# Expert rounds in narrow-wide pairs, with two small reorderings, in a one-core two-block transformer kernel

## The reference

```python
# first block, layer 0: hyena on 512 channels, order 2, by FFT-like convolutions
y_hy = hyena_mixer(z[..., :3 * C_HYENA], *hy)
# first block, layer 1: top 2 of 8 experts for each token
x = x + gt2 * moe_swiglu(modulate(rmsnorm(x, g_ffn), sh2, sc2), w_router[j], b_router[j],
                         moe_w1[j], moe_w3[j], moe_w2[j])
# second block, layer 0: retention, 4 heads of 512 values, normalised head by head
mu = jnp.mean(o, axis=-1, keepdims=True)
oc = o - mu
o = oc * lax.rsqrt(jnp.mean(oc * oc, axis=-1, keepdims=True) + EPS)
return (jax.nn.silu(g) * o) @ w_out
```

## Time and profile before

| | us |
|---|---|
| three runs | 2678.87, 2681.10, 2684.21 (median 2681.10) |
| the profiled execution's own time | 2679.57 |
| its span in the profile | 2677.8 |
| PE busy / DVE / ACT / POOL | 2458.1 / 1268.9 / 848.3 / 217.6 |
| transfers of expert weights | 340 of 1024 KB |

### The profile page before, as it was taken

The page is one execution under the profiler, slowest core; times in us unless marked ns, Lnnn a source line. Parts: engine busy times, 40 slices in busy tenths (PEclk is TensorE's granted clock), DMA queues, the critical chain, the costliest instruction groups (busy, mean ns, idle before and its releaser), DMA issues.

```text
span 2677.8 us, 39073 instructions
## 1 busy us (share of the span) xinstructions
PE 2458.1 (92%) x15909; PEld 1664.4 (62%) x15909; DVE 1268.9 (47%) x1936; ACT 848.3 (32%) x1213; POOL 217.6 (8%) x247
## 2 busy tenths in 40 slices
PE   7998999999887887889998998998989998899998
PEld 2864769954332322325776776777857996654996
DVE  3306645523310101005665755757455767895664
ACT  2101544421000000003554554554423544101553
POOL 0401200001000000000000000000000007362000
PEclk9998999999999999999998998999999999999999
DMA  8727275567999999998765765766556655534452
GB/s 297 172 79 266 26 260 176 187 265 281 382 411 412 410 414 409 411 414 302 260 229 188 255 220 191 265 207 219 190 218 209 218 187 179 199 126 134 158 184 84
DMA packets 248153, 648.75 MB, mean 242 GB/s; under 512 B 12623, under 2 KB 102896, under 8 KB 225656
## 3 DMA queue, kind: packets, MB, share of 16 engines
q10 hardware_dynamic: 111760, 358.68, 35.7%
q1 hardware_dynamic: 130648, 275.51, 29.7%
q0 software_dynamic: 5584, 12.28, 2.4%
HBM read 645.38 MB, written 1.05 MB: 241 GB/s over the span
## 4 chain that ended last, share of the span: by engine, by line
PE 75%; DMA 15%; DVE 6%; issue 2%; ACT 1%; POOL 1%; ACTq 1%; SPq 0%; POOLq 0%; DVEq 0%
DMA ring<-in_moe_w 13%; PE bank L1535 6%; PE bank L700 5%; PE bank L1553 5%; PE bank L1554 5%; PE bank L1552 5%; PE bank L702 4%; PE bank L701 4%; PE bank L1562 4%; PE bank L1563 4%; PE bank L1564 4%; PE bank L715 3%; PE bank L633 2%; PE bank L1596 2%; PE bank L667 2%; PE bank L1984 2%
## 5 line engine op out<-in xcount | busy, mean ns | idle before, releaser
L1074 DVE TENSOR_TENSOR w_low<-ring,w_high 128x1024 fp32r<-128x1024 f32 x252 | 305.5, 1224 | 129.0 <-ACT w_high L868 126.8
L633 PE MATMUL bank<-ring,arena 128*64 128x512 f32 (+1 forms) x1280 | 267.3, 548 | 71.1 <-DMA ring<-in_moe_w 71.1
L868 ACT ACTIVATE w_high<-ring 128x1024 fp32r<-128x1024 f32 x252 | 265.3, 1058 | 197.0 <-PE bank L702 195.4
L2459 DVE TENSOR_TENSOR ring_low<-ring,up_high 128x1024 fp32r<-128x1024 f32 x186 | 227.0, 1278 | 113.3 <-ACT up_high L2101 112.9
L1552 PE MATMUL bank<-ht_low,up_high 128*128 128x256 f32 x960 | 272.9, 284 | 0.0
L633 PEld LDWEIGHTS bank<-ring,arena 128*64 128x64 f32 x1280 | 81.9, 136 | 252.4 <-DMA ring<-in_moe_w 151.0
L2101 ACT ACTIVATE up_high<-ring 128x1024 fp32r<-128x1024 f32 x186 | 182.5, 1046 | 84.3 <-PE bank L1564 73.0
L1058 DVE TENSOR_TENSOR HT<-HT,bank 128x512 f32<-128x512 f32 (+1 forms) x20 | 12.4, 622 | 374.6 <-PE bank L633 374.6
L1553 PE MATMUL bank<-ht_high_cf_up,up_high 128*128 128x256 f32 x640 | 183.0, 286 | 0.0
L1552 PEld LDWEIGHTS bank<-ht_low,up_high 128*128 128x128 f32 x960 | 180.3, 188 | 1.6 <-DVE arena L2335 0.8
L1554 PE MATMUL bank<-ht_high_cf_up,ring_low 128*128 128x256 f32 x640 | 181.1, 283 | 0.0
(11 more groups left out here) (424 smaller groups left out, 4218.9 us busy)
## 6 DMA issues: line engine op xcount, KB each, us to landing
ring<-in_moe_w ACTq DMA_DIRECT2D x340, 1024.0 KB, 14.3
ring<-in_w_ada SPq DMA_DIRECT2D x48, 1024.0 KB, 7.7
ring<-in_ada_w SPq DMA_DIRECT2D x48, 1024.0 KB, 5.0
ring<-in_ffn_w_up SPq DMA_DIRECT2D x44, 1024.0 KB, 5.1
ring<-in_ffn_w SPq DMA_DIRECT2D x33, 1024.0 KB, 5.4
ring<-in_ret_w_in SPq DMA_DIRECT2D x24, 1024.0 KB, 5.2
ring<-in_ffn_w_down SPq DMA_DIRECT2D x22, 1024.0 KB, 4.9
ring<-in_w_in SPq DMA_DIRECT2D x12, 1024.0 KB, 11.2
```

The source lines that it names most:

```text
L633: mm = pe.matmul(PS[b][64 * n:64 * n + 64, 0:cols], XGF[:, ks * h + k, :], w[:, k, cols * n:cols * n + cols], start=h + k == 0, stop=ks * ...
L868: act.activation(WH[half % SPLIT][:, :], slot(moe_first + i)[:, HALF * (half % 2):HALF * (half % 2) + HALF], ACT.Copy)\
L1074: dve.tensor_tensor(out=WL[half % SPLIT][:, :], in0=slot(i)[:, HALF * (half % 2):HALF * (half % 2) + HALF], in1=WH[half % SPLIT][:, :], op ...
L2459: dve.tensor_tensor(out=low_of(base + tile, q), in0=slot(base + tile)[:, HALF * q:HALF * q + HALF], in1=high_of(part, n), op=ALU.subtract) ...
```

## The change

Three edits, whose lines are independent of each other.

1. `all_rounds` has a first loop of narrow rounds and a second one of pairs, each a narrow round and then a wide one. There are as many pairs as wide rounds (at least one), and the first loop takes the narrow rounds that remain (at least one). DVE computes positions for this order, with four more instructions, and its tables of rounds have 16 columns where they had 12. `narrow` gets a second argument m, the count of narrow rounds alone, for `hid_turned`, which only they raise.
2. Hyena: PE turns chunk by chunk, in the second order as each chunk is finished; the spectrum is announced in two halves (banks 2 and 4 first, then 3 and 5), DVE announces its products by halves, and the inverse transform adds the halves, with one bank for each chunk (2, 4, 6, 7), so that each chunk is announced alone.
3. Retention: DVE multiplies (o - mean) by the gate in one instruction per tile while ACT takes the root; ACT then scales by the reciprocal (two instructions per head). `ret_var` is raised twice per head, the second time with the reciprocal. PE's `mod_rows` of heads 0 and 1 stand behind the head's output, not ahead of it, and heads 2 and 3 wait for `ret_var` where they waited for `ret_gated`.

```diff
-        MAX_ROUNDS = E8 + SEQ * 2 // (FULL + 1)
+        MAX_ROUNDS = 1 + 2 * (E8 - 1)
...
-            with eng.Fori(0, n_narrow) as g:
-                narrow(g)
-            with eng.Fori(0, n_wide) as j:
-                wide(n_narrow + j, j)
-            return n_narrow + n_wide
+            with eng.Fori(0, n_first) as g:
+                narrow(g, g)
+            with eng.Fori(0, n_pairs) as j:
+                narrow(n_first + j * 2, n_first + j)
+                wide(n_first + j * 2 + 1, j)
+            return n_first + n_pairs * 2
...
-                            pe.wait_ge(sem("hid_turned"), g * MOE_CHUNKS + block_upto(s - 2))
+                            pe.wait_ge(sem("hid_turned"), m * MOE_CHUNKS + block_upto(s - 2))
...
-            link(dve.tensor_tensor(out=ROUND_N[:, 2:3], in0=n0, in1=n1, op=ALU.add))
-            link(dve.tensor_tensor(out=ROUND_N[:, 0:1], in0=ROUND_N[:, 2:3], in1=ROUND_N[:, 1:2], op=ALU.subtract))
-            link(dve.tensor_tensor(out=POS, in0=SUM0, in1=KIND0, op=ALU.mult))
-            link(dve.scalar_tensor_tensor(out=BYV, in0=SUM1, scalar=n0, in1=KIND1, op0=ALU.add, op1=ALU.mult))
+            link(dve.tensor_tensor(out=ROUND_N[:, 2:3], in0=n0, in1=pairs, op=ALU.subtract))
+            link(dve.tensor_scalar(first, ROUND_N[:, 2:3], 1.0, None, ALU.max))
+            link(dve.tensor_scalar(first_1, first, 1.0, None, ALU.add))
+            link(dve.scalar_tensor_tensor(out=POS, in0=SUM0, scalar=first_1, in1=SUM0, op0=ALU.subtract, op1=ALU.add))
+            link(dve.tensor_tensor(out=POS, in0=POS, in1=SUM0, op=ALU.max))
+            link(dve.tensor_tensor(out=POS, in0=POS, in1=KIND0, op=ALU.mult))
+            link(dve.scalar_tensor_tensor(out=BYV, in0=SUM1, scalar=first, in1=SUM1, op0=ALU.add, op1=ALU.add))
+            link(dve.tensor_tensor(out=BYV, in0=BYV, in1=KIND1, op=ALU.mult))
...
-                else:
-                    pe.wait_ge(sem("hy_out"), 4)
-                for t in range(TT):
-                    for c in range(4):
+                for c in range(4):
+                    if o:
+                        pe.wait_ge(sem("hy_out"), c + 1)
+                    for t in range(TT):
...
-                for i in range(4):
+                for i in (0, 2, 1, 3):
                     for t in range(TT):
                         mm = pe.matmul(bank(2 + i), DFTF[:, t, P * i:P * i + P], VT[:, t, :], start=t == 0, stop=t == 1)
-                mm.then_inc(sem("hy_spec"), 1)
+                    if i >= 2:
+                        mm.then_inc(sem("hy_spec"), 1)
                 mod_rows(sa, 0, 1 + o, 0, KD, 1)
...
+                for f in range(2):
+                    pe.wait_ge(sem("hy_prod"), 2 * o + f + 1)
+                    for c in range(4):
+                        for i in (f, 2 + f):
+                            mm = pe.matmul(PS[CONV_BANKS[c]][:, 0:SEQ], YF[:, i, P * c:P * c + P], IDFT[:, i, :], start=i == 0, stop=i == 3)
+                        if f:
+                            mm.then_inc(sem("hy_conv"), 1)
...
-                if h < 2:
-                    mod_rows(sbm, 2, 2, 4 * h, 4 * h + 4, 5)
                 pe.wait_ge(sem("ret_decayed"), h + 1)
                 if h >= 2:
-                    pe.wait_ge(sem("ret_gated"), 2 * (h - 1))
+                    pe.wait_ge(sem("ret_var"), 2 * (h - 1))
...
+                if h < 2:
+                    mod_rows(sbm, 2, 2, 4 * h, 4 * h + 4, 5)
...
+                act.wait_ge(sem("ret_var"), 2 * h + 2)
+                for t in range(TT):
+                    ch.step(act.activation(SG[:, t, h, :], SG[:, t, h, :], ACT.Identity, scale=grstd[:, t:t + 1]), sem("ret_gated"))
...
+                for t in range(TT):
+                    stt(SG[:, t, h, :], bank(2 * (h % 2) + t), bn2[:, t, 0:1], SG[:, t, h, :], ALU.subtract, ALU.mult)
                 dve.wait_ge(sem("ret_std"), h + 1)
-                link(dve.reciprocal(grstd, gstd))
+                link(dve.reciprocal(grstd, gstd), sem("ret_var"))
...
-                for t in range(TT):
-                    ts(RON, bank(2 * (h % 2) + t), bn2[:, t, 0:1], grstd[:, t:t + 1], ALU.subtract, ALU.mult)
-                    tt(SG[:, t, h, :], SG[:, t, h, :], RON, ALU.mult, sem("ret_gated"))
```

More of the change, by code:

```diff
@@ L328, in build @@
         NF = H[:, 1, :].rearrange("p (t k n) -> p t k n", t=TT, k=4)
+        CONV_BANKS = (2, 4, 6, 7)
         def score_bank(it):
@@ L620, in moe_tensor, with narrow @@
             mm.then_inc(sem("scattered"), 1)
-            def narrow(g):
+            def narrow(g, m):
                 def up(kind, s, b):
@@ L819, in load_ahead, with narrow @@
                 moe_load(act, now if i + AHEAD < NT else after, (i + AHEAD) % NT)
-            def narrow(g):
+            def narrow(g, _):
                 now, after = experts_of(g)
@@ L1707, in _ @@
                     pe.wait_ge(sem("qkv_ready"), 10)
-                else:
-                    pe.wait_ge(sem("hy_out"), 4)
-                for t in range(TT):
-                    for c in range(4):
+                for c in range(4):
+                    if o:
+                        pe.wait_ge(sem("hy_out"), c + 1)
+                    for t in range(TT):
                         mm = pe.transpose(PS[t][:, P * c:P * c + P], ZC[:, c, P * t:P * t + P], ident[:, :])
-                    mm.then_inc(sem("hy_turned"), 1)
+                        if c == 3:
+                            mm.then_inc(sem("hy_turned"), 1)
                 pe.wait_ge(sem("hy_vt"), 2 * (o + 1))
-                for i in range(4):
+                for i in (0, 2, 1, 3):
                     for t in range(TT):
                         mm = pe.matmul(bank(2 + i), DFTF[:, t, P * i:P * i + P], VT[:, t, :], start=t == 0, stop=t == 1)
-                mm.then_inc(sem("hy_spec"), 1)
+                    if i >= 2:
+                        mm.then_inc(sem("hy_spec"), 1)
                 mod_rows(sa, 0, 1 + o, 0, KD, 1)
-                pe.wait_ge(sem("hy_prod"), o + 1)
-                for c in range(4):
-                    for i in range(4):
-                        mm = pe.matmul(PS[6 + c // 2][:, SEQ * (c % 2):SEQ * (c % 2) + SEQ], YF[:, i, P * c:P * c + P], IDFT[:, i, :],
-                                       start=i == 0, stop=i == 3)
-                    mm.then_inc(sem("hy_conv"), 1)
+                for f in range(2):
[5 more added lines that the diff above has]
+                            mm.then_inc(sem("hy_conv"), 1)
             NA = TT * HEADS
@@ L2568, in _ @@
                     tt(YF[:, f, :], YF[:, f, :], T4[0], ALU.subtract)
[L2569 to L2572 removed]
+                    if f == 0:
+                        tt(YF[:, 2, :], YF[:, 2, :], T4[1], ALU.add)
+                        tt(YF[0:1, 0, :], PS[2][0:1, :], KS[0:1, o, 0, :], ALU.mult)
+                        tt(YF[0:1, 2, :], PS[4][0:1, :], KS[0:1, o, 2, :], ALU.mult, sem("hy_prod"))
+                    else:
+                        tt(YF[:, 3, :], YF[:, 3, :], T4[1], ALU.add, sem("hy_prod"))
                 mod_ready(sa, 0, 1 + o, 1)
                 for c in range(4):
[L2575 to L2576 removed]
+                    dve.wait_ge(sem("hy_conv"), 4 * o + c + 1)
+                    y = PS[CONV_BANKS[c]][:, 0:SEQ]
                     tmp = T4[c % 2][:, 0:SEQ]
```

24 lines of the change are left out of this document (10 added, 14 removed).

## The result

| | us |
|---|---|
| before, median of four runs (lowest to highest) | 2682.1 (2678.9 to 2684.2) |
| changed, median of four runs | 2651.0 (2648.9 to 2653.6) |
| ratio, 95% interval | 0.989, 0.9878 to 0.9903 |
| forecast, range | 2660, 2645 to 2675 |
| the changed kernel's profiled execution, its span | 2649.67, 2647.9 |

The kernel became 31 us faster where 21 were forecast. The side and the range held, and most single terms did. But the experiments show a cause of about 10 us, a third of the whole, that the forecast had no term for, and it has nothing to do with the order of the work.

The account below looks back on a forecast made before the run. Narrow rounds were taken as bound by transfers, wide ones by PE. Terms -11.5 - 4.3 + 1.6 - 5.1 - 1.6 = -20.9 took the profiled 2679.57 to 2658.7, given as 2660 against the median; range 2645 to 2675.

Parts of the forecast that it names:

- N-W for W-W: Expert rounds: two wide rounds now follow a narrow one instead of a wide one, each 5.8 us shorter, -11.5 us.
- W-N for N-N: Expert rounds: two narrow rounds now follow a wide one instead of a narrow one, 104.9 against 107.05 us each, -4.3 us.
- the stall: Narrow round after a wide one: the loop's branch back was taken to cost 3.0 us.
- the round at the full clock: Narrow round after a wide one: taken as 100.1 us, like the first narrow round, which also began with full slots.
- The 1.8 for the low clock: Narrow round after a wide one: PE starts at the low clock, so the first tile comes free about 1.8 us later.
- Routing: Routing ahead of the expert rounds: four more DVE instructions and larger tables, all on the path, +1.6 us.
- Hyena: Hyena convolutions: delivery by halves and chunks removes PE's waits for DVE before the inverse transforms, -5.1 us.
- attention, whose first DVE work followed at once: Attention behind hyena: its first DVE work follows at once, so the whole 5.1 us gained is kept.
- Retention: Retention heads: shorter DVE chain for head 1, first ret_out product sooner, -1.6 us.
- 1 (the pause used in full): Narrow rounds after wide ones: full ring, no branch stall or low clock, 97 us each, 2644 us in all; chance 0.13.
- 2 (the pause not used): Narrow rounds after wide ones start with four tiles ready, 112.6 us each, +15, 2675 us in all; chance 0.12.
- 3: Hyena and retention give nothing, since each wait removed exposes the next one: 2667 us; chance 0.13.
- 4: Narrow rounds after a wide one stay at the low clock, 180 us for 104.9, 2810 in all; chance 0.05 together with another rival.

Follow-up runs that it names:

- E4: The kernel before with only the retention head loop changed, arena at its old place: 2677.5 us, ratio 0.9998.
- E2: The kernel before with only the new order of rounds and its routing, small_i 24 columns wide: 2656.7 us, ratio 0.9912.
- E5: The changed kernel with small_i 32 columns wide instead of 24: 2647.7 us, ratio 0.9885.
- E11: The changed kernel as it is, run once more: 2648.1 us, ratio 0.9884.
- E12: The changed kernel with small_i 32 columns wide and 14 unused filling matmuls in PE's first waits of attention: 2644.6 us, ratio 0.9878.
- E7: The changed kernel with the wide round first in each pair and the routing table to match: 2655.1 us, ratio 0.9914.
- E1: The kernel before with small_i 24 columns wide instead of 16, nothing else: 2669.4 us, ratio 0.9964.
- E3: The kernel before with only the hyena part changed, arena at its old place: 2676.4 us, ratio 0.9984.
- E6: The changed kernel with small_i 40 columns wide instead of 24: 2650.7 us, ratio 0.9893.
- E9: The changed kernel with small_i 48 columns wide instead of 24: 2648.2 us, ratio 0.9879.

## Why the prediction was right, and where it was not

- **N-W for W-W, -11.5**: right in kind, too small. The wide rounds add up to 575.1 for 589.0, -13.9. The second and third went from 198.3 to about 191.9 (-6.4 each, forecast -5.8), and even the first, which followed a narrow round before too, from 192.4 to 191.2: its gather ran at the full clock (3.70 us for 4.14), its first product came after 6.9 us for 7.3, and the low clock behind it lasted 6.8 us for 10.2. The forecast took the one measured border, 192.4, as the value. In the nine profiles with the new order such rounds took 191.0 to 192.6, so 192.4 is near the upper edge; E4, whose rounds are those of before, has 190.9 for its first one.
- **W-N for N-N, -4.3**: right, with its working. 104.7 and 104.8 against 104.9; over E2, E5, E11 and E12 the eight such rounds took 103.3 to 105.8. Its pieces nearly hold one by one: the stall 3.39 and 3.29 (3.0 taken), the round at the full clock 99.6 to 100.8 in E7 (100.1 taken). The 1.8 for the low clock, which the forecast gave without its working, came out smaller: behind the stall the rounds took 101.3 and 101.6, 1.2 to 1.5 over the 100.1. The two errors cancel.
- **Routing, +1.6**: 36.0 us before from the router's first matmul to the first narrow one, 36.8 after, +0.8; the lower bound.
- **Hyena, -5.1**: the steps up to attention were right or cautious. The inverse transform of order 2 started at 242.2, counted from order 1's spectrum 45.9 us later for 50.3, and attention's scores came at 252.9 for 256.5. The step that failed is "attention, whose first DVE work followed at once", hence all of it kept. PE's waits there drop its clock, which is back no sooner than before (263.0 before, 262.8 to 264.9 in the seven profiles with the new hyena and no filling). The low stretches add up to 10.2 us with the new hyena and before, but before 3.4 of them lay in the inverse transform (in E1 and E2 too), and now all lie in attention. From the inverse transform of order 2 to the ffn's first product it took 125.6, 126.6, 126.1 and 127.3 us with the old hyena (before, E1, E2, E4) and 127.9, 126.9, 128.1, 126.9, 128.0, 128.0 and 127.3 with the new one (changed, E3, E5, E6, E7, E9, E11), a mean of 1.2 more, where the earlier scores alone should have made it 1.3 less. Counted from the start of the run, the ffn's first product is at 371.9 in the mean of the four and at 368.4 in that of the seven. So about 3.5 us arrive, and the time of E3 says -4.3. A single pair of profiles can hide this: in the first two it is at 370.10 and 370.07.
- **Retention, -1.6**: -1.95 in every profile that has it.
- **Missing**: the width of `small_i`. The description of the change leaves this line out, and the forecast, which goes through the change part by part, gave the eight columns no cost and no name. E1 puts -9.6 on them. Without them the changed kernel would stand near 2661, where the forecast was 2660. By the stages it is -18.2 (rounds), +0.8, -4.3, -1.95 and -9.6, -33 in all; by the measured times -31. That the time fell into the range all the same is luck in part: the range was made wide for rivals 1 and 2, which did not come true, and that width took in a term which it did not know.
- **Rivals**: 1 (the pause used in full) fell to the stall and the low clock, though E7 shows its mechanism, a narrow round of 100 us. 2 (the pause not used) fell: the three slots fill from 1188 on. 3 fell with E3 and E4's profiles. 4 fell: the clock is back after 3.4 and 6.8 us in the two narrow rounds behind a wide one. The Trainium skill ("TensorE: Matmul & The Clock Gate", Loop structure matters more than you think) speaks of a long wait for DMA between every matmul and the next, which leaves PE at the low clock. The narrow rounds, with some 0.6 us of waiting at each tile of several matmuls, are no such loop, and they were granted 0.98 and above. Attention, with waits of 2.5 and 1.2 us for DVE and ACT, is none either, and there the clock did fall to 0.50.

## What to carry to other kernels

A change that resizes any tensor moves everything allocated behind it, and PE's pace can depend on that: before crediting an edit, run the kernel before with nothing but the new size. A loop whose body no longer fits what the engine holds of its code pays at each branch back; put ahead of the branch what the next round can use (here a full ring) and behind it the round that is bound by something other than PE. When a wait on PE is shortened or moved, follow the granted clock behind it until it is back: the gain is what is left then.

## What the runs showed of the hardware

- Moving one buffer by 32 bytes changed PE's pace in 256-column fp32r products by 2.7% (121.3 to 118.1 ns from start to start), reproducible to 0.1 ns in kernels with different code, while those of 512 columns, L1562 to L1564 x264 (394, 396 and 393 ns before), stayed within 2 ns in E1. The first product has only its stationary operand in the arena and went from 284 to 282, the third only its moving one and went from 283 to 278, so both play a part or one is charged to the other; which stays open.
- The branch back cost 0, 2.9 to 3.6 or 4.7 to 4.8 us by what the loop's body and the target were, and each stall has a 16 KB transfer of instructions in it. A wide gather behind it ran 7.04 us for 3.70: the clock fell in the stall (low from 1191.5 to 1208.6 in E7, with the stall from 1189.2 to 1194.0).
- Two executions of the changed kernel differ by 2.0 us at the first inverse transform already (213.01 and, in E11, 211.00), and the stretch from the end of the first conv-ffn to the end of the run differs by 5.2 between E1 and E2 (404.3 and 409.5), which have the same code there. That is why terms of 2 us were read here from stages and not from the total.
